# Products that nobody reads, put into five places of TensorE's queue in one decode-and-prompt step of a hybrid trunk with 32 experts

## The reference, cut to what matters

```python
z = rms_norm(x) @ w_in                       # one projection, split between the two groups
m_out, C, n, m = mlstm_mix(mq, mk, mv, mo, ...)
a_out = attn(aq, ak, av, rel_bias, sinks)
y = x + concat([m_out, a_out]) @ w_out
xn = rms_norm(y)
gates, experts = softmax(top_k(xn @ w_router + b_router, 4))
h = (clip(xn @ w_up[e] + b_up[e]) + 1) * swish(min(xn @ w_gate[e] + b_gate[e], 7))
y = y + sum_over_4(gate * (h @ w_down[e] + b_down[e]))
return rms_norm(y, final_norm), states, caches
```

## Time and profile before

| | us |
|---|---|
| median of three runs (lowest, highest) | 1519.29 (1518.84, 1520.31) |
| the profiled execution | 1518.44 |
| its span, first to last instruction | 1516.7 |
| PE busy in the span | 1447.8 (95%) |
| DVE busy | 1273.2 (84%) |
| ACT busy | 1054.7 (70%) |
| mean granted clock of TensorE | 0.965 |

### The profile page before, as it was taken

One profiled execution on the slowest core, in us unless ns is written; L12 is line 12 of the kernel. 1 busy time (PEld: TensorE's weight loads), 2 busy tenths in 40 slices (PEclk: granted clock), 3 DMA queues, 4 the chain that ended last, 5 costly groups with the idle time before them and its releaser, 6 DMA issues.

```text
span 1516.7 us, 21417 instructions
## 1 busy us (share of the span) xinstructions
PE 1447.8 (95%) x7157; PEld 1062.5 (70%) x7157; DVE 1273.2 (84%) x1234; ACT 1054.7 (70%) x961; POOL 180.5 (12%) x186
## 2 busy tenths in 40 slices
PE   6999997878999999999999999999999999999993
PEld 5999865755777777777777777777777777777772
DVE  4344466369999999999999999999999999999995
ACT  4454443356787878777777878787878777777875
POOL 3000131142000001110000000000001110000000
PEclk9999997668999999999999999999999999999997
DMA  7311222149999999999999999999999999999994
GB/s 229 119 56 56 80 95 92 47 161 350 381 378 377 371 374 371 375 368 370 363 376 378 374 377 376 371 371 377 374 373 372 368 368 371 366 373 375 387 357 158
DMA packets 170596, 464.78 MB, mean 306 GB/s; under 512 B 14228, under 2 KB 28192, under 8 KB 170288
## 3 DMA queue, kind: packets, MB, share of 16 engines
q1 hardware_dynamic: 157240, 430.99, 76.4%
q0 software_dynamic: 8880, 24.00, 7.0%
q10 hardware_dynamic: 4440, 9.36, 1.8%
HBM read 447.90 MB, written 23.59 MB: 311 GB/s over the span
## 4 chain that ended last, share of the span: by engine, by line
PE 91%; DVE 4%; ACT 1%; issue 1%; ACTq 1%; DVEq 1%; DMA 1%; POOLq 0%; SPq 0%
PE ps L1738 87%; PE ps L1741 4%; DMA acc_rows<-reg_a,pass_tok 0%; ACT ring L1136 0%; DVE reg_w L1466 0%; DVE reg_z L1543 0%; DVE ring L1159 0%; DVE ring_r L1179 0%; DVE ring L1729 0%; DVE ring_r L1170 0%; DVE ring L1443 0%; DMA ring<-acc_rows 0%; DVE reg_b L1439 0%; DVE reg_b L1338 0%; DVE reg_z L1393 0%
## 5 line engine op out<-in xcount | busy, mean ns | idle before, releaser
L1738 PE MATMUL ps<-ring_r,reg_z_r 128*96 128x512 f32 x4608 | 1097.7, 395 | 0.0
L1738 PEld LDWEIGHTS ps<-ring_r,reg_z_r 128*96 128x96 f32 x4608 | 736.9, 162 | 308.9
L1063 ACT ACTIVATE ring_r<-ring 128x2048 fp32r<-128x2048 f32 x387 | 736.3, 1915 | 169.8 <-PE ps L1738 167.6
L451 DVE TENSOR_TENSOR ring_r<-ring,ring_r 128x2048 fp32r<-128x2048 f32 x355 | 797.7, 2284 | 51.2 <-ACT ring_r L1063 51.1
L730 POOL DMA_INDIRECT acc_rows<-reg_a,pass_tok x32 | 48.8, 1525 | 1004.5 <-ACT reg_a L1080 884.0
L1738 PE MATMUL ps<-reg_a_r,ring_r 128*128 128x264 f32 (+1 forms) x576 | 110.1, 286 | 0.0
L1738 PE MATMUL ps<-ring_r 128*128 128x256 f32 (+3 forms) x372 | 102.4, 324 | 0.0
L1738 PEld LDWEIGHTS ps<-reg_a_r,ring_r 128*128 128x128 f32 x576 | 90.6, 188 | 2.4 <-issue 2.2
L1086 ACT ACTIVATE reg_z_r<-ps 128x384 fp32r<-128x384 f32 x130 | 58.8, 479 | 37.8 <-PE ps L1741 37.8
L1666 DVE TENSOR_TENSOR ring_r<-ring,ring_r 128x1024 fp32r<-128x1024 f32 x64 | 77.7, 1213 | 0.0
L1738 PEld LDWEIGHTS ps<-ring_r 128*128 128x128 f32 (+1 forms) x372 | 68.0, 185 | 7.8 <-issue 0.5
(11 more groups left out here) (324 smaller groups left out, 951.2 us busy)
## 6 DMA issues: line engine op xcount, KB each, us to landing
ring<-in_w_gate SPq DMA_DIRECT2D x131, 1024.0 KB, 7.7
ring<-in_w_up SPq DMA_DIRECT2D x128, 1024.0 KB, 6.2
ring<-in_w_down SPq DMA_DIRECT2D x128, 1024.0 KB, 8.9
ring<-in_w_in SPq DMA_DIRECT2D x9, 1024.0 KB, 6.6
ring<-in_w_out SPq DMA_DIRECT2D x4, 1024.0 KB, 5.2
ring<-in_x_prompt SPq DMA_DIRECT2D x4, 512.0 KB, 8.6
reg_a<-in_x_prompt SPq DMA_DIRECT2D x4, 512.0 KB, 6.2
xhat_rows<-reg_w ACTq DMA_DIRECT2D x4, 512.0 KB, 2.7
```

What stands on the lines that cost most here:

```text
L451: return eng.tensor_tensor(rest_r(k), w, rounded_r(k).bitcast(F32), ALU.subtract)
L1063: act.activation(rounded_r(k), ring[:, slot_of(k), :], ACT.Copy).then_inc(hi_ready, 1)
L1738: return pe.matmul(out, lhsT, rhs, start=start, stop=stop, skip_group_check=True)
```

## The change

A new helper, `keep_warm(n, bank, rest)`, issues n products into a PSUM bank that is not in use. Nothing reads what they write. It is called four times, and a fifth place issues 24 products of the identity with itself directly. There are no new waits or semaphores; DVE, ACT, POOL and SP have the same instructions in the same order as before.

```diff
+            def keep_warm(n, bank, rest=False):
+                w = piece_hi(N_IN)
+                for _ in range(n):
+                    if rest:
+                        mm(ps[bank][0:96, 0:512], gT_r[:, 0:96], e_bias_r[2][:, 0:512])
+                    else:
+                        mm(ps[bank][:, 256:512], w[:, 0:P], w[:, 256:512])
...
             pe.wait_ge(ident_made, 1)
+            for _ in range(24):
+                mm(ps[6][:, 0:P], ident[:, :], ident[:, :])
             for i in range(NTILE):
...
             mm(ps[2][:, 0:130], r4, r32[:, 0:130]).then_inc(sample_pe, 1)
+            keep_warm(40, 4)
             for h in range(MH):
                 pe.wait_ge(hn_ready, h + 1)
...
             mm(ps[2][0:32, 256:386], g4, part2).then_inc(sample_pe, 1)
+            keep_warm(10, 7)
             project(0)
...
+            keep_warm(20, 7, rest=True)
             pe.wait_ge(count_ready, 2)
             transpose_rows(0, 16)
+            keep_warm(8, 0, rest=True)
             pe.wait_ge(ybias_ready, 2 * NTILE)
```

## The result

The changed kernel takes 1523.41 us (median of 20 runs, 1520.83 to 1527.6), the kernel before 1518.96 us (median of 20 runs beside them, 1516.5 to 1522.42). The ratio is 1.003, with a 95% interval of 1.0023 to 1.0037: slower by 4.5 us, 3.5 to 5.6.

A forecast was written before the change was run, and what follows sets the result against it. PE was taken to set the pace from 352 us to the loop's end. From the profiled 1518.44 us, 0 + 0 + 1.2 (project(1)) + 4.1 (gathered rows and loop entry) gave 1523.7 us, range 1520.3 to 1528.3.

The forecast's parts named there:

- place 4: 20 products ahead of the gathered rows' transposes: they stand on the path, +6.1 us (5.5 to 7.1); transposes give 0.7 back.
- Place 1: 24 identity products at the start: gain 0, since tile 2's square waits for its DMA; at most 1.2 us.
- Places 2 and 3: 40 and 10 products around the heads' transposes: project(0) 2.7 us faster, hidden behind DVE, so 0.
- project(1) at a lower clock: Idle time behind the faster project(0) lets the clock fall, so project(1) loses 1.2 us (0 to 2.7).
- place 5: Eight products behind the gathered rows' transposes: 1.9 us inside a 2.24 us wait, 0 (at the lower level +1.2).
- The loop's entry: Expert loop entered at the higher clock: its first 7 products take 1.6 us instead of 2.7 to 2.9, -1.3 us.
- Nothing comes back in the loop: PE sets the expert loop's pace, so whatever moves its entry moves the end by as much.
- All fillers in waits: All five places lie in waits and every faster burst pays: 1513.2 us, chance 0.05.
- Part given back: project(0)'s 2.7 us reach the end (1519.8), or the loop catches up a late entry (about 1519); chance together 0.17.
- The filler does not lift the clock: Gathered rows' 96-row products leave the clock low: 8.6 us for 20, +9.8, with project(1) 1529.4 us; chance 0.08.
- a rival for places 2 and 3: Clock falls during the heads' transposes; project(0) and project(1) run as before, sum 1.2 us less; no chance given.

The follow-up runs named there:

- p1_identity: Kernel before plus only the 24 identity products at the program's start: 1519.56 against 1518.19 us, ratio 1.0006.
- p23_heads: Kernel before plus only the 40 and 10 products around the memory heads' transposes: 1520.75 against 1518.19 us, ratio 1.0019.
- p4_rows: Kernel before plus only the 20 products ahead of the gathered rows' transposes: 1523.82 against 1518.19 us, ratio 1.0038.
- p5_rows: Kernel before plus only the 8 products behind the gathered rows' transposes: 1517.89 against 1518.19 us, ratio 1.0.
- no4: Changed kernel without the 20 products ahead of the gathered rows' transposes: 1519.52 us against 1519.54 for the kernel before, ratio 1.0005.
- p4_double: Changed kernel with 40 instead of 20 products ahead of the gathered rows' transposes: 1530.16 us against 1519.54 for the kernel before, ratio 1.0073.
- p23_behind: p23_heads plus 22 products behind project(0), ahead of project(1): 1520.14 us against 1519.34 for the kernel before, ratio 1.0003.
- fill_ks: Kernel before plus only 24 products of 256 columns behind project(2), in PE's wait: 1516.59 against 1519.34 us, ratio 0.9987.
- moved: Kernel before plus only ten 96-row products in PE's waits before the gathered rows land: 1517.93 against 1519.54 us, ratio 0.9993.
- ks_p5_r: ks_p5 plus six products of 256 columns in route(1)'s wait: 1515.92 us against 1518.86 for the kernel before, ratio 0.9987.
- ks_p5: fill_ks plus the 8 products behind the gathered rows' transposes: 1516.67 us against 1518.86 for the kernel before, ratio 0.9992.

## Why the prediction was right

It said 1523.7 us, slower; measured were 1523.41 us, slower by 4.5 us where it had 4.4 against the median. The mechanism that decides, place 4 on the path, is shown. That the two numbers agree to 0.1 us is luck: the gathered rows cost 0.6 us more than the sum had, project(1)'s 1.2 us are not in the changed kernel's profile, and the measured difference itself is known only to 1 us. Point by point, by its steps:

- **Place 1, 0.** Right, and for its reason: the square at 13.16 us behind tile 2's DMA. The identity products ended at 9.2 us for 9.5. The first steps met the lower clock again, though in the changed kernel for 1.4 us instead of 2.9. The bound of -1.2 us for a gain was not reached; p1_identity leaves -0.5 to +2.3.
- **Places 2 and 3, 0 with a hidden gain.** Right: project(0) was faster by 2 to 2.8 us and project(1) not earlier, in the changed kernel and in p23_heads. One of its signs did not come: project(0) was to run at the higher level and began at the lower in the changed kernel.
- **project(1) at a lower clock, +1.2 (0 to 2.7).** Open. In the changed kernel's own profile the term was 0 (granted clock 1.00 from 256.5 to 272.3 us), so the idle time did not bring the clock down there. In p23_heads it was 0.8, but 0.9 and 1.0 in p4_rows and p5_rows, without the places. The runs say 1 to 4.6 us for places 2 and 3 together, and -0.6 to 2.1 with places 1 and 5 beside them (no4). 1.2 lies in both, which does not show that it is project(1)'s clock.
- **Place 4, +6.1 (5.5 to 7.1).** The changed kernel shows 7.12 - 0.82 = 6.30 us. The transposes, the wait and place 5 together gave 0.88 back, where 0.7 was put for the transposes and 0 for place 5.
- **The loop's entry, -1.3.** Too large: 36.88 to 36.19, 0.7 us; in p5_rows 1.0. In p5_rows the first 50 products take the whole 1.3 us less (11.55 us for 12.87, starts to starts). In the changed kernel PE, now at the higher clock, stands at the second piece of weights: its first product starts 0.49 us behind the one before, at 359.47 us, where 0.23 is usual, and DVE's rest of that piece (L451) is done at 359.42. The prediction left DVE's rests out of this term. Another 0.2 (changed kernel) to 0.4 us (p5_rows) is lost further on, ahead of the second expert. So the stage's sum is +4.73 for the predicted +4.1, in its bounds of 3.5 to 5.1.
- **Nothing comes back in the loop.** Right: the 1102.1 us behind the second expert are the same whether PE comes 2.8 or 11.4 us later.
- **The rivals.** *All fillers in waits* falls with p4_rows and no4. *Part given back* falls with p4_double's 4.45 us in the stage, and with project(1)'s start. *The filler does not lift the clock* falls with the rise at 350.4 us during it.

The Trainium skill's rule that transposes do not count for the clock ("TensorE: Matmul & The Clock Gate", Part 4: PE-mode transpose) was a rival for places 2 and 3: the clock would fall during the heads' transposes, and project(0) would run as before. The first half came in four of the five profiles with these places: in the changed kernel, no4, p4_double and p23_behind the clock fell between the two groups of transposes (at 241.2 us in the changed kernel), and only in p23_heads it stayed at 1.00 from 229.0 to 256.2 us. The second half did not: project(0) took 5.81 to 6.59 us in all five, against 8.60 before. At the start of the program the profiles do not agree either. In the nine without place 1, the first 16 transposes are all that PE has done, and tile 2's then ran fast in four (1.10 to 1.21 us for eight, the kernel before among them) and slow in the other five (1.97 us for eight where all are recorded). So the prediction's argument against the rule, which rests on the kernel before alone, is weaker than it reads; no run was made to settle the rule. The Trainium skill's advice against long idle gaps ("TensorE: Matmul & The Clock Gate", Why this matters for your kernels) holds here with a condition: filling a gap was worth 2 us where the burst behind it was waited for (fill_ks), and nothing where DVE hid the burst (project(0) in places 2 and 3).

## What to carry to other kernels

Products that nobody reads are worth something only where PE really waits and where someone is waiting for the burst behind, and only if the clock is then at its higher level (in moved it was not): read from the timeline the idle time ahead of the burst, and from the chain who sets the start of what comes after it. A filler in front of work that could have started (place 4) costs its own duration; one in front of a burst that is hidden (places 2 and 3) turns the burst's gain into idle time ahead of the next burst. A filler longer than its wait at the lower clock (place 5: 3.0 us for 2.2) is paid at once and earns later.

## What the runs showed that was not expected

- **The same instructions take up to 4 us more or less between project(1) and `down_bias(4)`.** The changed kernel, no4 and p4_double have identical instructions up to there, and took 89.48, 89.49 and 93.44 us. The kernel before, p1_identity, p4_rows and p5_rows share theirs too, and took 91.07, 89.46, 90.87 and 91.01 us. The profile shows the clock as what differs: here the same window of the changed kernel and of p4_double.

```profile
258.00:270.00 12.00, 11.26 (x66) 9.54 (x65) 5.39 (x24) 4.81 (x11) 0.00 (x0) 1.00 0.07 25
```

```profile
258.00:270.00 12.00, 11.26 (x56) 9.46 (x55) 3.47 (x16) 4.70 (x10) 0.00 (x0) 0.78 0.09 31
```

PE is busy for 11.26 us in both, and gets 66 or 56 matmuls done. So two single profiles can differ by 2.9 us where the medians differ by 4.5, and a term of 1 us on the clock needs the stage's own length and not the total.

- **Being busy did not lift the clock.** In moved PE was busy for 9.46 of 10.6 us ahead of the gathered rows' transposes, and the granted clock stayed at 0.50 to 353.8 us; in the changed kernel it rose 4.5 us after the start of 22 products without a gap. What of the two differs for the clock was not tried.
- **A few products may hold it; this is not shown.** Six products in 0.8 us of waiting in `route(1)` went with a clock of 1.00 up to 293.6 us (ks_p5_r), where it fell at 279.9 and 279.5 without them (fill_ks, ks_p5). But these are single profiles, and the clock had been at 0.50 from 266.4 to 269.7 us in ks_p5_r alone.
